# Forget rows of the cached tokens, loaded once per head and added on TensorE, in a hybrid decoder step

## The reference

```python
def fox_sample(q, k, v, logf, k_past, v_past, logf_past):
    d_new = lax.cumsum(logf, axis=1).transpose(0, 2, 1)
    rev = (lax.cumsum(logf_past, axis=1, reverse=True) - logf_past).transpose(0, 2, 1)
    sp = jnp.einsum('bqhd,bkhd->bhqk', q, k_past) * scale
    sp = sp + d_new[:, :, :, None] + rev[:, :, None, :]
    ...
    p = jax.nn.softmax(jnp.concatenate([sp, sn], axis=-1), axis=-1)
    out = p[..., :n_past] @ v_past + p[..., n_past:] @ v
```

## Time and profile before

| | |
|---|---|
| median of 3 runs | 2051.61 us (2049.55 to 2056.92) |
| the profiled execution | 2061.25 us, span 2059.6 us |
| TensorE busy | 1900.0 us, 92% |
| VectorE busy | 831.9 us, 40% |
| ScalarE busy | 442.7 us, 21% |
| mean granted clock of TensorE | 0.964 |
| HBM read, written | 432.44 MB, 32.17 MB |

### The profile page before, as it was taken

One profiled execution on the slowest core, in us unless ns is written; L12 is line 12 of the kernel. 1 busy time (PEld: TensorE's weight loads), 2 busy tenths in 40 slices (PEclk: granted clock), 3 DMA queues, 4 the chain that ended last, 5 costly groups with the idle time before them and its releaser, 6 DMA issues.

```text
span 2059.6 us, 33477 instructions
## 1 busy us (share of the span) xinstructions
PE 1900.0 (92%) x12402; PEld 1123.7 (55%) x12402; DVE 831.9 (40%) x1867; ACT 442.7 (21%) x1021; POOL 262.5 (13%) x402
## 2 busy tenths in 40 slices
PE   6999989888799999999999899994999999999994
PEld 5677555555378868888874467543333333333331
DVE  5644476777365523333344505344111111111115
ACT  3111133434301011111010124231222222122223
POOL 0203333233300000000000000000111111111120
PEclk9999999999889999999999999997999999999997
DMA  7759999999821140120121204019899999999966
GB/s 258 262 172 345 388 340 359 332 325 319 277 82 52 52 154 11 52 62 11 51 74 62 85 1 153 21 76 361 303 382 384 376 372 375 371 378 372 365 234 258
DMA packets 207019, 458.56 MB, mean 223 GB/s; under 512 B 18625, under 2 KB 48338, under 8 KB 206730
## 3 DMA queue, kind: packets, MB, share of 16 engines
q1 hardware_dynamic: 174282, 357.89, 48.7%
q0 software_dynamic: 32576, 98.53, 13.4%
HBM read 432.44 MB, written 32.17 MB: 226 GB/s over the span
## 4 chain that ended last, share of the span: by engine, by line
PE 79%; DVE 6%; DMA 5%; issue 4%; ACT 3%; DVEq 1%; POOLq 1%; SPq 1%; POOL 0%; ACTq 0%
PE ps L1276 17%; PE ps L1572 11%; PE ps L1603 6%; PE ps L1327 6%; PE ps L1583 5%; PE ps L1105 5%; PE ps L1356 5%; PE ps L1120 3%; PE ps L1612 3%; PE ps L1077 3%; PE ps L1445 2%; PE ps L1208 2%; PE ps L1228 2%; DMA vpage<-in_cache_v 2%; DMA kraw<-in_cache_k 1%
## 5 line engine op out<-in xcount | busy, mean ns | idle before, releaser
L1572 PE MATMUL ps<-gu,xgT 128*64 128x512 f32 x1024 | 226.8, 595 | 0.9 <-ACT xgT L1917 0.9
L2100 DVE STREAM_TRANSPOSE kt<-kraw 128x1024 f32<-128x1024 f32 x128 | 151.1, 1219 | 45.3 <-DMA kraw<-in_cache_k 36.6
L1276 PE MATMUL ps<-xnT,ring 128*128 128x264 f32 x672 | 161.9, 392 | 0.9 <-issue 0.9
L2929 POOL DMA_DIRECT2D vpage<-in_cache_v x232 | 124.6, 537 | 288.6 <-PE ps L1228 223.3
L2816 DVE TENSOR_TENSOR sig_a<-ps,sig_a 128x256 f32<-128x256 f32 x32 | 13.6, 424 | 324.9 <-ACT sig_a L1921 324.9
L1276 PEld LDWEIGHTS ps<-xnT,ring 128*128 128x128 f32 x672 | 129.4, 193 | 25.6 <-issue 3.1
L1572 PEld LDWEIGHTS ps<-gu,xgT 128*64 128x64 f32 x1024 | 70.6, 137 | 131.9 <-issue 128.8
L1603 PE MATMUL ps<-wd,hidT_a 128*64 128x512 f32 x512 | 120.3, 612 | 17.3 <-ACT hidT_a L1927 10.6
L1583 PE MATMUL ps<-gu,xgT 128*32 128x512 f32 x1024 | 115.8, 592 | 0.0
L1105 PE MATMUL ps<-xnT,early 128*128 128x352 f32 x320 | 102.6, 477 | 3.9 <-DVE xnT L2044 3.9
L1105 PEld LDWEIGHTS ps<-xnT,early 128*128 128x128 f32 x320 | 61.4, 196 | 38.4 <-issue 9.3
(11 more groups left out here) (441 smaller groups left out, 2966.6 us busy)
## 6 DMA issues: line engine op xcount, KB each, us to landing
kraw<-in_cache_k SPq DMA_DIRECT2D x256, 256.0 KB, 5.0
gu<-in_w_expert_gate SPq DMA_DIRECT2D x32, 2048.0 KB, 20.1
gu<-in_w_expert_up SPq DMA_DIRECT2D x32, 2048.0 KB, 24.9
wd<-in_w_expert_down SPq DMA_DIRECT2D x31, 2048.0 KB, 21.4
vpage<-in_cache_v POOLq DMA_DIRECT2D x232, 256.0 KB, 5.2
ring<-in_w_in SPq DMA_DIRECT2D x12, 1024.0 KB, 8.9
yy<-y_d SPq DMA_DIRECT2D x16, 512.0 KB, 10.2
early<-in_w_in SPq DMA_DIRECT2D x6, 1024.0 KB, 11.5
```

Of the source, the lines that this page charges most:

```text
L1276: last = nc.tensor.matmul(bank(R.bank(name, f, q))[:, 0:QT], weight[:, k], src[:, k, cols], start=k == 0, stop=k == HK - 1)
L1572: last = nc.tensor.matmul(bank(0)[h * BA:(h + 1) * BA, :].rearrange("p (x n) -> p x n", x=2), src[:, k, 0:BA], weight[:, k, :, h * DE // 2 ...
L2100: last = nc.vector.transpose(kt[n % 2].rearrange("p c e s -> p (c e s)")[:, x * 1024:(x + 1) * 1024], kraw[n % 2].rearrange("p c d -> p (c ...
L2929: pool.dma_start(vpage[value_place(n)][:, p, :], t["cache_v"][ds(page, 1)].rearrange("a s d -> (a s) d")).then_inc(v_in[value_place(n)], 16)
```

## The change

The tile `rev` gets 32 rows in place of 128, so that `load_rev` brings each row of `rev_d` once; the two tiles lie in rows 0 to 31 and 32 to 63 of `rev_pair`. `load_rev` waits for the sort product of unit 8 (b - 2) + 7 and no longer for its reader on VectorE. A new tile `to_queries` (two copies of 32 rows x 128 columns, made once from the identity by VectorE) holds a 1 where a column (page, head, query) belongs to a row (page, head). `sort_scores` leaves its four products open, waits for `rev_in` and adds a fifth product into the same bank, which spreads each row of `rev` over its four queries. `join_scores` waits for `rev_in` no longer and adds a zero in place of `rev`.

```diff
+        zero = new("zero", [P, 1])
...
-        rev = [at(f"rev{p}", [P, SU * PAGE], w + p * 4096) for p in range(2)]
+        rev_pair = at("rev_pair", [8 * H, SU * PAGE], w)
+        rev = [rev_pair[p * 4 * H:(p + 1) * 4 * H] for p in range(2)]
+        to_queries = at("to_queries", [8 * H, P], w + 4096)
...
             def load_rev(b):
                 if b >= 2:
-                    R.read(sp, "sp", (b - 2) * SU + SU - 1)
+                    R.made(sp, "sp", (b - 2) * SU + SU - 1)
                 sp.dma_start(rev[b % 2], rev_d.rearrange("g h x -> (g h) x")[:, b * SU * PAGE:(b + 1) * SU * PAGE]
-                             .unsqueeze(1).to_broadcast([4 * H, DS, SU * PAGE])).then_inc(rev_in[b % 2], 16)
+                             ).then_inc(rev_in[b % 2], 16)
...
             def sort_scores(n):
+                b, u = n // SU, n % SU
                 R.read(pe, "sq", n)
                 R.pe_free(pe, "sp", n)
                 for g in range(4):
-                    last = nc.tensor.matmul(bank(3)[g * QH:(g + 1) * QH, 0:PAGE], ident[:, g:P:4], sraw[n % 2], start=True, stop=True)
-                last.then_inc(R.full, 1)
+                    nc.tensor.matmul(bank(3)[g * QH:(g + 1) * QH, 0:PAGE], ident[:, g:P:4], sraw[n % 2], start=True, stop=False)
+                pe.wait_ge(rev_in[b % 2], 16 * (b // 2 + 1))
+                nc.tensor.matmul(bank(3)[:, 0:PAGE], to_queries[b % 2 * 4 * H:(b % 2 + 1) * 4 * H], rev[b % 2][:, u * PAGE:(u + 1) * PAGE], start=False, stop=True
+                                 ).then_inc(R.full, 1)
...
+            nc.vector.memset(zero, 0.0)
...
+            for p in range(2):
+                rows = slice(p * 4 * H, (p + 1) * 4 * H)
+                nc.vector.tensor_copy(to_queries[rows].rearrange("k (r q) -> k r q", q=DS),
+                                      ident[rows, rows].unsqueeze(2).to_broadcast([4 * H, 4 * H, DS]))
             for p in range(2):
                 nc.vector.memset(qblk[p], 0.0)
...
             def join_scores(n):
                 b, u = n // SU, n % SU
-                if u == 0:
-                    dve.wait_ge(rev_in[b % 2], 16 * (b // 2 + 1))
                 R.made(dve, "sp", n)
                 nc.vector.tensor_tensor_reduce(out=sprob[b % 2][:, u * PAGE:(u + 1) * PAGE], in0=bank(3)[:, 0:PAGE],
-                                               in1=rev[b % 2][:, u * PAGE:(u + 1) * PAGE], scale=1.0, scalar=-3e38,
+                                               in1=zero[:, 0:1].to_broadcast([P, PAGE]), scale=1.0, scalar=-3e38,
                                                op0=ALU.add, op1=ALU.max, accum_out=tops[:, b, u:u + 1]).then_inc(R.by["dve"], 1)
```

## The result

The changed kernel takes 2072.24 us (median of 6 runs, 2063.98 to 2078.52) against 2054.27 us of the kernel before on the same chip (6 runs, 2048.8 to 2059.31). The ratio is 1.0064, with an interval of 1.0041 to 1.0088: 8 to 18 us slower, 13 us at the middle. The two medians stand 18.0 us apart, at the upper end of that interval. Every ratio is to the kernel before on the same chip; one execution of it at 2840 us, in a slow state, is left out of those of experiments 9 and 10. The forecast was 2071 us, 19.3 us slower. The median came out almost exactly and the direction holds, but a step of 19.3 us lies just above the interval of the ratio: the later forty products were priced too high, the first 24 too low, and neither of the two credits is seen.

A forecast was written before the change was run, and what follows sets the result against it. TensorE was taken to bound the stage to 241 us, then TensorE mixed with transfers and waits. 2.6 + 3.0 + 8.6 + 8.6 - 1.5 - 2.0 = 19.3 us over 2051.61 gave 2071 us, range 2050 to 2088 us.

The forecast's parts named there:

- the later forty products: Sorts after 241 us: 14.4 us added, 16 of 40 covered by TensorE's waits, 8.6 us paid (0 to 19.2).
- the first 24: Sorts up to 241 us, where TensorE alone sets the pace: all paid, 24 x 0.36 = 8.6 us (5.3 to 11.5).
- the two credits: Time taken off the sum: 1.5 us for smaller `rev` transfers and 2 us for a less lowered TensorE clock.
- The wait moves: First sort, near 83 us: TensorE instead of VectorE waits for the first `rev`, 2.6 us (0.5 to 3.7).
- The 3.0 us for the clock: Behind the first sort's wait: work lost to a lower TensorE clock, 3.0 us (0 to 3.4).
- The price of the product: Fifth product in each sort: 0.22 us stream, 0.12 us shape change, with the wait instruction 0.36 us (0.22 to 0.48).
- The transfers: Eight `rev` loads cut to 128 KB: room for key and value pages, 1.5 us won (0 to 7.4).
- Given back: TensorE's clock from 253 us on: fewer gaps lose less clock, 2 us won (0 to 16).
- rival 3: After 241 us, pages come in time and TensorE's gaps close, restoring the clock: 11 us faster, 2040 us; chance 0.08.
- three signs of being wrong: Slot growth of 0.2 us or less or 0.5 or more; `rev` landing before 83.3 us; 250-515 us clock near 1.00.
- Rival 1: After 241 us nearly all 40 products vanish in waits and `rev` lands early: 6.4 to 8.4 us, 2059 us; chance 0.26.
- Rival 2: Products cost 0.48 us, three quarters paid after 241 us, whole start stall and clock: 33 us, 2085 us; chance 0.14.

The follow-up runs named there:

- experiment 9: The changed kernel, unedited, timed and profiled a second time; ratio to the kernel before 1.0054 (1.0037 to 1.0072).
- experiment 10: The kernel before with only TensorE's wait for `rev` added ahead of each sample's first sort, no fifth product, loads of 512 KB; ratio 1.0021 (1.0006 to 1.0036).
- experiment 4: The changed kernel with the first load of `rev` issued before the keys of unit 3, first timing; ratio 1.0068 (1.0044 to 1.0092).
- experiment 11: The changed kernel with the first load of `rev` issued before the keys of unit 3, timed again; ratio 1.0043 (1.0025 to 1.0062).
- experiment 6: The changed kernel with the spreading as four 128x32 products and the first `rev` load before the keys of unit 3; ratio 1.0021 (1.0004 to 1.0039).
- experiment 5: The changed kernel with the spreading done as four 128x32 products, `rev` tiles of 128 rows zero-filled below the loaded 32; ratio 1.0047 (1.0027 to 1.0066).
- experiment 7: The changed kernel with the fifth product made twice, weights 0.5 in place of 1; ratio 1.0136 (1.0112 to 1.0159).
- experiment 2: The changed kernel with the fifth product only for page groups 0 to 23, forget rows left out for the others; ratio 1.0052 (1.0034 to 1.007).
- experiment 8: The kernel before, unedited, timed and profiled a second time; ratio 1.0002 (0.9984 to 1.0021).
- experiment 3: The changed kernel with the fifth product only for page groups 24 to 63, forget rows left out for the others; ratio 1.0015 (0.9999 to 1.0031).
- experiment 1: The changed kernel without the fifth product and TensorE's wait for `rev`, smaller loads and zero operand kept; ratio 0.9998 (0.998 to 1.0016).

## Why the prediction was right, and where it was off

**The wait moves.** Forecast 2.6 us, measured 2.03 and 1.99 us. Forecast landing 85.9 us, measured about 85.3 us. The 3.0 us for the clock were right as a size and not as a certainty: 0 in one profile of the changed kernel, 3.3 us in the other, 2.6 us in experiment 10. That the wait is paid is shown by experiment 10 in the kernel before. In the changed kernel itself the timings of experiments 4 and 11 leave it open; their profiles, and experiment 6 against 5, speak for it.

**The price of the product.** Forecast 0.36 us from a stream of 0.22 us and 0.12 us for one change of shape; measured 0.42 us = 0.21 + 0.21 us, shown by experiments 5 and 7 on either side. The change of shape was mis-sized: I halved L1232's 0.23 us, and nearly all of it was due. That 0.23 us is itself a remainder and depends on the rate taken for the stream: 0.22 us for 128 columns was forecast, 0.21 us measured. Why one more change behind the sort costs as much as the two around L1232 was not tried. The Trainium skill, TensorEngine Tiling (Array Packing), "Key Properties", has changes of the tiling mode drain TensorE and gives no figure; experiment 5, which has none within the sort, agrees. The Trainium skill, TensorE: Matmul & The Clock Gate, "Why this matters for your kernels", states that one product over 32 rows takes as long as one over 128. The trace agrees as far as it goes: the added stream of 32 rows in experiment 7 and the four concurrent ones of 128 rows in experiment 5 both take 0.21 us.

**The first 24 slots are paid.** Forecast 8.6 us with 0.36 us each, measured 10.1 us at 0.42 us, with 10.7 us of time for them and a start wait of 1.1 us in experiment 2.

**The later forty.** Forecast 8.6 us paid of 14.4; measured 3.1 us of 16.8 when they stand alone (at most some 6 us by the interval). The changed kernel's two ratios are 0.4 and 2.5 us over that of experiment 2, with intervals of about 5 us, and its second part of the stage is 2 to 4 us longer, once 6.5 us. This is the step that was off most. I counted as cover only the waits that do not start from TensorE's transposes, 16 of 40; some four fifths of the added work vanished. Where it went is seen in the windows from the 24th sort to the reload, experiment 8 against experiment 3:

```profile
240.76:547.52 306.76, 266.96 (x3328) 160.47 (x3320) 214.84 (x629) 120.76 (x313) 107.92 (x201) 0.97 0.94 334
```

```profile
239.57:548.82 309.25, 279.24 (x3408) 171.01 (x3400) 215.39 (x629) 120.40 (x313) 108.21 (x201) 0.98 0.93 326
```

The second is 2.5 us longer. TensorE's idle time fell from 39.8 to 30.0 us: in these windows the waits for pages and keys went from 8.3 to 1.8 us and those for `diag` from 9.4 to 7.2 us, 8.7 of the 9.8 us. The rest of the 16.8 us, 4.5 us, is neither length nor idle time; the clock, 0.98 on average against 0.97, would be some 3 us of it (an estimate from two rounded means). So the kinds of wait that I counted as cover were the right ones; their share was not. I set the number of such waits against the number of products; set in time, there were 17.7 us of them for 16.8 us of products. That a product shortens the next such wait even some slots later is argued from this and not traced. Experiment 7 shows the cover getting thinner and not its end.

**The transfers.** Forecast 1.5 us won; experiment 1 shows 0.4 us, with an interval of 4 us to either side. 3.1 MB less moved nothing that can be measured.

**Given back, 2.0 us for the clock.** Not supported as it was priced: the clock of 0.66 at 253 us, on which the term and rival 3 rested, was of one execution. The 0.01 or so by which the clock is higher behind the 24th sort with the forty products is already in their 3.1 us.

**The sum.** 2.0 (start) + 0 to 3.3 (its clock) + 10.1 (first 24) + 3.1 (later forty) = 15.2 to 18.5 us, against 13.1 and 11.1 us by the two ratios, each with an interval of about 4 to 5 us to either side. Of the forecast's 19.3 us the later forty were 5.5 us too dear and the start 0.6 us; the first 24 were 1.5 us too cheap, and the 3.5 us taken off for transfers and clock were not won. With the 3.0 us for the start's clock left as they are, that leaves 18.2 us: the errors nearly cancel, and that is luck. The mechanism was right in its direction, in the moved wait and in the first 24 slots; the cover of the later forty was not. The measured median stood 18.0 us over that of before, the ratio says 13.1; so the forecast median, 2071 us, is nearer to the measured one, 2072.24 us, than the size of the step was to the ratios. None of the three signs of being wrong came: the slot grew by 0.42 us, `rev` landed at about 85.3 us, and the clock from 263 to 515 us was 0.97 and 0.96.

**The rivals.** Rival 1 had the cover nearly right and the price of a slot and the start too low; it gave 6.4 to 8.4 us. With the measured 2.0 and 10.1 us, its 0 to 2 us for the later forty and nothing won by the transfers it gives 12 to 14 us, nearer to the ratios than the forecast: as a mechanism it is the better description of this kernel. Rival 2 needed three quarters of the later forty paid, which is refuted. Rival 3 said faster, which the result refutes. Experiment 1 shows why: with the smaller loads and no product, TensorE still waits 5.7 + 1.8 us for pages of values from 253 to 515 us, no less than before (5.2 us and, in experiment 8, 4.9 + 1.4 us).

What stays open: between the reload of `xnT` and the end the changed kernel's first profile is another 5.7 us longer than the first one before (1513.4 against 1507.7 us). The second profiles are 1511.1 and 1508.0 us, experiment 7, which has more of the change, 1505.5 us, and all the profiles lie between 1502.3 and 1513.4 us. Two of one kernel (4 and 11) differ by 3.3 us. So part of it at least can be the spread of single executions; no experiment aimed at it.

## What to carry to other kernels

Ask who adds a value for nothing now. VectorE read the sort's result from PSUM in any case, and one more operand was free there; the same sum on the engine that sets the pace cost 0.42 us 64 times, and the bytes saved had been waited for once, off the path. If a small product must go in between column-tiled ones, give it their shape, even with zero rows: it halves the price. And before a stall is priced from one profile, take a second of the same kernel: at the first sort of the changed kernel the wait repeated (2.03 and 1.99 us), the clock behind it did not. Cutting a stage at the point where its limit changes told more here than the total time: for the doubled product the total pointed to 64 paid slots, the two parts to 24 paid ones and a longer start.

## What the runs showed of the hardware

A product of float32 over 128 columns in a 32x128 tile between products in 128x32 and 128x128 tiles costs 0.42 us, of which 0.21 us is the change of shape; four concurrent products of 128x32 behind four like them cost 0.21 us. VectorE's sum and maximum out of PSUM takes between about 240 and 293 ns in every kernel; its median was 253, 254 and 273 ns in the three profiles with the `rev` tile as operand and 274 to 292 ns in the profiles with the zero column. Whether the operand does that was not tried, and 64 times 38 ns, 2.4 us, had no effect that experiment 1 could show. A wait of TensorE of 2.0 us was followed by the full clock in one execution (2.4 GHz, 16 records in 5.00 us) and by the lower level (1.2 GHz) for some microseconds in another (8.00 us). The waits of 1.05 us (experiment 2), 1.08 us (8), 1.65 us (10) and 1.81 us (3) were followed by the full clock, those of 2.13 us (first profile before), 3.17 us (5), 3.38 us (7) and 3.40 us (10) by the lower one.
